# Ten of twelve turns of whole activations moved from TensorE to VectorE blocks and transfers through device memory

## The chip, the core and the metric

The kernel runs on one core of one Trainium2 chip. The metric is the device time of one execution in microseconds (us), the median of three runs. Beside it stands one profiled execution, from which all rows below come. The core has five engines with a queue each: TensorE (PE; its weight loads are PEld), VectorE (DVE), ScalarE (ACT), GpSimd (POOL) and SyncE (SP). Sixteen DMA engines serve the transfers that SP and ACT issue.

## The reference

One encoder layer on x of 256 tokens by 2048 channels, all in f32:

```python
h      = rms_norm(x, g_mix)
z, xbc, dt_f, dt_b, q, k, v, gate_a, gate_b = split(h @ w_in)
y_ssm  = mamba2_bidir(...)        # scans, times silu(z), grouped rms_norm, 2048 channels
y_attn = attention(rope(rms_norm(q)), rope(rms_norm(k)), v)
merged = sigmoid(gate_a) * (y_ssm @ w_ssm_up) + sigmoid(gate_b) * (y_attn @ w_attn_up)
x      = x + merged @ w_out
x      = x + square(relu(rms_norm(x, g_mlp) @ w_mlp_in)) @ w_mlp_out
out    = rms_norm(x, g_final)
```

## The kernel before

**Windows and pieces.** Each product with a weight matrix is cut into windows of 512 output columns. A window has 8 pieces; a piece is 2 of the 16 tiles of 128 input channels. A piece of weights (512 KB) is loaded by SP from device memory into one of 4 slots of `raw` (7 slots in the MLP), split by ACT into a rounded high part `whi` (L637) and by DVE into the rest `wlo` (L1022), and used by PE in three passes (L1719 to L1721) for each of the two blocks of 128 tokens. ACT splits three pieces ahead of PE (`LEAD_HI`), DVE two (`LEAD_LO`). ACT may split into a slot only once PE is done with the piece four before. SP may load into a slot of `raw` once DVE has split what lay there. So all engines keep step with PE piece by piece, with a lead of some pieces.

**Work beside the windows.** `walk` writes out by hand which other work is done beside each window. A function such as `zgate(p, j, ...)` exists once for every engine and is called after piece `p` of the window on that engine, so what it waits for also holds up the weight splits queued behind it on that engine.

**The turns.** PE needs the activations with channels on partitions, while a product gives tokens on partitions. So a whole activation of 256 by 2048 is turned in four rounds of 512 channels. There are three such activations, twelve rounds:

- rounds 0 to 3 (`TS_Z`), in `zgate`: y times silu(z), beside the windows z 1, z 2, z 3 and k;
- rounds 4 to 7 (`TS_MERGED`), in `merged`: the gated sum of the branches, beside attn_up 1, 2, 3 and out 0;
- rounds 8 to 11 (`TS_X2`), in `residual`: the new x, beside out 1, 2, 3 and the first mlp_in window.

A round is eight transposes of 128 by 128 on PE (`transpose_round`, L1740) into the two banks 0 and 1 of the PSUM tensor `S`; then ACT makes the high part out of `S` (`split_high`, L661 and L666) and DVE the low part (`split_low`, L1059 and L1066). The semaphores are `ts_t`, `ts_hi`, `ts_lo`. A consumer window waits on `ts_lo`; the windows out 0 and mlp_in (0, 0) are `late`: they begin with the four channel tiles of the last round missing and wait for that round only before piece 6.

`transpose_round` is also used for q and k in `rope`, for the first conv groups and, in another form, for the attention weights. These stay as they are.

Of the kernel before, what the change touches and what calls it, by code (L numbers as in the profile page):

```python
# [61 lines left out]
FIN_CUTS = (0, 640, FIN, 1664)  # L62

TS_Z, TS_MERGED, TS_X2, TS_END = 0, 4, 8, 12


def walk(eng, window):

    window(0, 0, "xbc", 0, [("rates", 0)])
    window(0, 1, "gate", 0, [("conv", 0), ("decays", 0)])  # L70
    window(1, 0, "xbc", 1, [("scan", 0), ("gate", 0)])
    window(1, 1, "gate", 1, [("conv", 1), ("tables", 0)])
    for i in range(2, GROUPS):
        window(i, 0, "xbc", i, [("gate", i - 1), ("scan", i - 1)])
        window(i, 1, "gate", i, [("conv", i)])
    window(8, 0, "z", 0, [("scan", 7), ("gate", 7)])
    window(8, 1, "z", 1, [("zgate", 0)])
    window(9, 0, "z", 2, [("zgate", 1)])
    window(9, 1, "z", 3, [("zgate", 2)])
    window(10, 0, "k", 0, [("zgate", 3)])  # L80
    window(10, 1, "v", 0, [("rope", 0)])
    window(11, 0, "q", 0, [("values", 0)])
    window(11, 1, "q", 1, [("rope", 1)])
    window(12, 0, "q", 2, [("rope", 2)])
    window(12, 1, "q", 3, [("rope", 3)])
# [12 lines left out]
    window(19, 0, "mlp_in", (0, 0), [("residual", 3)])  # L98

    def pair(g, q, before):  # L100
        window(4 * g + 21 + q, 0, "mlp_pair", (g, q, 0), before)
        window(4 * g + 21 + q, 1, "mlp_pair", (g, q, 1), [("mix_out", (g, q))])

    for g in range(4):
        if g:
            window(4 * g + 19, 0, "mlp_in", (g, 0), [("sums", g - 1), ("mixed", (g - 1, 0))])
        for j in range(1, 4):
            window(4 * g + 19 + j // 2, j % 2, "mlp_in", (g, j), [("hidden", (g, j - 1))] + (
                [("mixed", (g - 1, 1))] if g and j == 1 else []))
# [152 lines left out]
def build(nc, x, x_t, w_in, w_dt, gains_in, taps_in, rows_in, w_ssm_up, w_attn_up, w_out, w_mlp_in, w_mlp_out,  # L262
# [130 lines left out]
    assert top[0] <= nc.sbuf_usable_end, (top[0], nc.sbuf_usable_end)  # L393
    squares_end = nc.alloc_sbuf_tensor_at("squares_end", [P, TB, D], F32, offset=region_a)
    top[0] = region_r
    m_acc1 = nc.alloc_sbuf_tensor_at("m_acc1", [P, 4, N], F32, offset=top[0])
    g_last = place("g_last", [P, D])
    region_f = top[0]
# [42 lines left out]
    expo = sem("expo")  # L441

    ts_t, ts_hi, ts_lo = sem("ts_t"), sem("ts_hi"), sem("ts_lo")
    x_hi, x_lo = sem("x_hi"), sem("x_lo")
    sq_x, var_x, rstd_x = sem("sq_x"), sem("var_x"), sem("rstd_x")
    xt_sq, xt_sum, xt_mm = sem("xt_sq"), sem("xt_sum"), sem("xt_mm")
# [94 lines left out]
        return BLOCK[N_MLP + 8 * PIECES * g + 4 * PIECES + 2 * PIECES * q + PAIR_ORDER[q].index((unit, 3)) + 1]  # L541

    cum_rows = nc.dram_tensor("cum_rows", (2, HEADS, T), F32).ap()

    block = keep.enter_context(nc.Block())

# [85 lines left out]
    def _(act):  # L632
# [6 lines left out]
        def split(m):  # L639
# [13 lines left out]
                act.wait_ge(t_made, turn + SUM_TURN[block])  # L653
            high_part(m, n)

        def split_high(rnd, dst, k0, gain=None, factor=1.0):

            act.wait_ge(ts_t, rnd + 1)
            if gain is None:
                for c in range(2):  # L660
                    last = act.activation(dst[:, ds(k0 + 2 * c, 2), :],  # L661
                                          S[:, c, :].rearrange("p (c t) -> p c t", c=2), ACT.Copy,
                                          scale=factor)
            else:
# [163 lines left out]
        def zgate(p, j, pr, pp):  # L828
            if p == 0:
                act.wait_ge(used, done(pr, pp))  # L830
                if j:
                    act.wait_ge(ts_t, TS_Z + j)
                else:
                    act.wait_ge(off_mm, GROUPS)
                for tb in range(TB):
# [12 lines left out]
            if p == 7:  # L848
                split_high(TS_Z + j, b_hi, 4 * j, gain=2)

        def rope(p, n, pr, pp):
# [59 lines left out]
                last.then_inc(taken[pp], 1)  # L911

        def merged(p, j, pr, pp):
            if p == 2:
                split_high(j + TS_MERGED, b_hi, j * 4, factor=0.5)

        def residual(p, j, pr, pp):
            if p == 2:
                split_high(TS_X2 + j, a_hi, 4 * j, gain=1)
# [59 lines left out]
        table = {f.__name__: f for f in (rates, decays, conv, scan, gate, zgate, rope, values, attend, merged,  # L979
                                         residual, hidden, finish)}  # L980
        between_splits = {f.__name__: f for f in (carry_out, mix_out)}

# [36 lines left out]
    def _(dve):  # L1019
# [7 lines left out]
        def split(m):  # L1027
# [23 lines left out]
            if i > 3:  # L1051
                low_part(m, n + i - 3)

        def split_low(rnd, hi, lo, k0, gain=None, factor=1.0):

            dve.wait_ge(ts_hi, rnd + 1)
            if gain is None:
                for c in range(2):
                    last = dve.scalar_tensor_tensor(  # L1059
# [249 lines left out]
        def zgate(p, j, pr, pp):  # L1309
# [22 lines left out]
            if p == 7:  # L1332
                split_low(TS_Z + j, b_hi, b_lo, 4 * j, gain=2)

        def rope(p, n, pr, pp):
# [13 lines left out]
            if p == 2:  # L1349
                dve.wait_ge(r_root, 2 * (n + 1))  # L1350
                if first(n):
                    dve.wait_ge(ts_t, TS_MERGED)
                else:
                    dve.wait_ge(r_t, n)
                for tb in range(TB):
# [77 lines left out]
        def merged(p, j, pr, pp):  # L1433
            if p == 0:
# [2 lines left out]
                if j == 0:  # L1437
                    dve.wait_ge(r_t, 5)
                else:
                    dve.wait_ge(ts_t, j + TS_MERGED)  # L1440
                dve.tensor_tensor(tmp_b[:, :, :], gates[:, 4 + j, :, :], gates[:, j, :, :], ALU.add
                                  ).then_inc(merge_v, 1)
            if p == 2:
                split_low(j + TS_MERGED, b_hi, b_lo, j * 4, factor=0.5)

        def add_product(j, pr, pp, bank):
# [7 lines left out]
        def residual(p, j, pr, pp):  # L1454
            if p == 0:
                add_product(j, pr, pp, lambda tb: out_product(j, tb))
            if p == 2:
# [98 lines left out]
        def finish(p, j, pr, pp):  # L1556
# [16 lines left out]
        table = {f.__name__: f for f in (rates, decays, conv, scan, tables, zgate, rope, attend, gated_a, merged,  # L1573
                                         residual, hidden, sums, mixed, mix_out, finish)}

        def window(r, par, kind, idx, sides):
# [136 lines left out]
    def _(pe):  # L1713
# [28 lines left out]
            return last  # L1742

        def split_round(rnd, src):
            if rnd:
                pe.wait_ge(ts_lo, rnd)
            transpose_round(src).then_inc(ts_t, 1)


# [104 lines left out]
                                        st_hi[:, 1 - c, :], st_lo[:, 1 - c, :], True, True)  # L1854
                last.then_inc(off_mm, 1)

        def zgate(p, j, pr, pp):
            if p == 6:
                pe.wait_ge(z_v, (j + 1) * Z_V)
                if j == 0:  # L1860
                    pe.wait_ge(scan_v, SCAN_V * GROUPS)
                split_round(TS_Z + j, lambda c, tb: tmp_a[:, tb, c * P:(c + 1) * P])

        def rope(p, n, pr, pp):
            if p == 6:
                pe.wait_ge(r_v, (n + 1) * ROPE_V)
                if n == 0:
                    pe.wait_ge(ts_lo, TS_MERGED)
                else:
                    pe.wait_ge(r_lo, 2 * n)  # L1870
                if n == 4:
# [38 lines left out]
                weigh(p - 4)  # L1910

        def merged(p, j, pr, pp):
            if p == 1:
                pe.wait_ge(merge_v, j + 1)
                pe.wait_ge(at_exp, 8 * KVH)
                split_round(j + TS_MERGED, lambda c, tb: tmp_b[:, tb, c * P:(c + 1) * P])

        def residual(p, j, pr, pp):
            if p == 1:
# [10 lines left out]
        table = {f.__name__: f for f in (rates, decays, conv, scan, zgate, rope, attend, merged, residual)}  # L1930

        def last_window(r, par, idx):

# [99 lines left out]
        def window(r, par, kind, idx, sides):  # L2033
# [139 lines left out]
```

## Time and profile before

| | us |
|---|---|
| median of 3 runs | 1622.51 (1622.29 to 1622.76) |
| span of the profiled execution | 1620.0 |
| PE busy | 1608.5 |
| DVE busy | 1264.1 |
| ACT busy | 917.1 |
| share of the 16 DMA engines, SP's queue | 58.4% |

The profiled execution's own rows cover its span, 1620.0 us from its first to its last instruction; the runs' median is 2.5 us above it. "Busy" of PE is modelled for pipelined matmuls, so it says that PE has work queued and not that it runs at its peak. The DMA share is the mean over the core's sixteen engines.

### The profile page before, as it was taken

The page shows a single profiled execution, that of the slowest core. Times are in us where ns is not written, and L with a number is a line of the kernel's source. Part 1 is how long each engine was busy: PE and PEld are TensorE (multiplying, and loading weights), DVE is VectorE, ACT ScalarE, POOL GpSimd, SP SyncE. Part 2 cuts the span into 40 slices and gives each one's busy share as a digit, 9 for nine tenths or more (in the row PEclk, how much of TensorE's full clock was granted, in tenths as well). Part 3 has the DMA queues.
Part 4 walks back from the last instruction along what each step waited for, and adds up shares of the span by engine and source line. Part 5 has one row for each costly group of instructions (what it writes and reads, how often), then busy time and mean ns, then how long its engine had stood idle before and what let it go on. Part 6 is the DMA issues. An engine that isn't in the chain of part 4 may idle for free.

```text
span 1620.0 us, 20751 instructions
## 1 busy us (share of the span) xinstructions
PE 1608.5 (99%) x8104; PEld 1362.2 (84%) x8104; DVE 1264.1 (78%) x1520; ACT 917.1 (57%) x1262; POOL 79.1 (5%) x67
## 2 busy tenths in 40 slices
PE   9999999999999999999999999999999999999998
PEld 7888888888888888888888888888888888888886
DVE  7888878888666677776665576999799988998893
ACT  6666556666565445544444555665556556655562
POOL 3000000000001134000000000000000000000000
PEclk9999999999999999999999999999999999999999
DMA  7666665666556664445576676458646764586471
GB/s 272 202 200 190 189 200 189 208 195 203 183 186 182 191 187 153 142 145 175 187 229 195 225 236 187 144 182 285 184 125 224 262 190 134 194 282 209 148 245 53
DMA packets 134194, 312.21 MB, mean 193 GB/s; under 512 B 9744, under 2 KB 10448, under 8 KB 133968
## 3 DMA queue, kind: packets, MB, share of 16 engines
q1 hardware_dynamic: 129376, 302.21, 58.4%
q10 hardware_dynamic: 4720, 8.68, 2.0%
q8 instruction: 64, 1.05, 0.3%
q14 instruction: 34, 0.28, 0.0%
HBM read 308.68 MB, written 2.16 MB: 192 GB/s over the span
## 4 chain that ended last, share of the span: by engine, by line
PE 96%; DVE 2%; issue 1%; ACT 0%; POOL 0%; DMA 0%; POOLq 0%; DVEq 0%
PE G L1719 17%; PE G L1720 17%; PE G L1721 17%; PE G L1728 13%; PE S L1728 7%; PE G L1732 6%; PE S L1719 4%; PE S L1721 4%; PE S L1720 4%; PE S L1732 4%; PE S L1740 1%; PE S L1847 1%; DVE wlo L1022 1%; PE S L1891 0%; PE S L1824 0%
## 5 line engine op out<-in xcount | busy, mean ns | idle before, releaser
L637 ACT ACTIVATE whi<-raw 128x1024 fp32r<-128x1024 f32 x395 | 417.0, 1059 | 418.1 <-PE G L1721 254.9
L1022 DVE TENSOR_TENSOR wlo<-raw,whi 128x1024 fp32r<-128x1024 f32 x395 | 482.5, 1236 | 128.7 <-ACT whi L637 127.4
L1719 PE MATMUL G<-whi,a_both 128*128 128x512 f32 x768 | 301.3, 392 | 2.3 <-DVE wlo L1022 1.7
L1721 PE MATMUL G<-whi,a_both 128*128 128x512 f32 x768 | 299.5, 390 | 0.0
L1720 PE MATMUL G<-wlo,a_both 128*128 128x512 f32 x768 | 299.5, 390 | 0.0
L1728 PE MATMUL G<-a_both,whi 128*128 128x512 f32 x640 | 201.7, 397 | 0.0
L1719 PEld LDWEIGHTS G<-whi,a_both 128*128 128x128 f32 x768 | 144.3, 188 | 33.3 <-issue 2.6
L1721 PEld LDWEIGHTS G<-whi,a_both 128*128 128x128 f32 x768 | 144.2, 188 | 30.1
L1720 PEld LDWEIGHTS G<-wlo,a_both 128*128 128x128 f32 x768 | 144.3, 188 | 28.7
L1732 PEld LDWEIGHTS G<-a_both,wlo 128*128 128x128 f32 x640 | 120.3, 188 | 28.2
L1719 PE MATMUL G<-whi,b_hi 128*128 128x512 f32 x342 | 133.9, 392 | 0.0
L1720 PE MATMUL G<-wlo,b_hi 128*128 128x512 f32 x342 | 133.6, 391 | 0.0
L1721 PE MATMUL G<-whi,b_lo 128*128 128x512 f32 x342 | 133.3, 390 | 0.0
L637 ACT ACTIVATE whi_late<-raw 128x1024 fp32r<-128x1024 f32 x85 | 88.9, 1058 | 67.2 <-PE S L1732 22.0
L1732 PE MATMUL G<-a_both,wlo 128*128 128x256 f32 x640 | 125.9, 278 | 0.0
L1022 DVE TENSOR_TENSOR wlo_late<-raw,whi_late 128x1024 fp32r<-128x1024 f32 x85 | 102.6, 1221 | 24.7 <-ACT whi_late L637 24.1
L637 ACT ACTIVATE whi_late<-gates 128x1024 fp32r<-128x1024 f32 x67 | 70.0, 1056 | 49.7 <-PE G L1732 17.9
L1728 PEld LDWEIGHTS G<-a_both,whi 128*128 128x128 f32 x640 | 97.6, 189 | 0.1
L1022 DVE TENSOR_TENSOR wlo_late<-gates,whi_late 128x1024 fp32r<-128x1024 f32 x67 | 81.1, 1221 | 18.7 <-ACT whi_late L637 18.6
L637 ACT ACTIVATE whi<-gates 128x1024 fp32r<-128x1024 f32 x63 | 66.2, 1056 | 38.2 <-PE G L1732 13.9
L1022 DVE TENSOR_TENSOR wlo<-gates,whi 128x1024 fp32r<-128x1024 f32 x63 | 76.3, 1222 | 12.5 <-ACT whi L637 12.0
L1728 PE MATMUL G<-a_both,whi_late 128*128 128x512 f32 x256 | 80.5, 396 | 0.0
(306 smaller groups left out, 2692.4 us busy)
## 6 DMA issues: line engine op xcount, KB each, us to landing
raw<-in_w_in SPq DMA_DIRECT2D x208, 512.0 KB, 4.3
raw<-in_w_mlp_in SPq DMA_DIRECT2D x74, 512.0 KB, 4.0
raw<-in_w_mlp_out SPq DMA_DIRECT2D x74, 512.0 KB, 5.0
gates<-in_w_mlp_in SPq DMA_DIRECT2D x54, 512.0 KB, 4.0
gates<-in_w_mlp_out SPq DMA_DIRECT2D x54, 512.0 KB, 4.9
raw<-in_w_ssm_up SPq DMA_DIRECT2D x32, 512.0 KB, 3.8
raw<-in_w_attn_up SPq DMA_DIRECT2D x32, 512.0 KB, 4.6
raw<-in_w_out SPq DMA_DIRECT2D x32, 512.0 KB, 4.6
```

Source lines behind the costliest of these rows:

```text
L637: act.activation(high(m), piece(n), ACT.Copy).then_inc(hi_made, 1)
L1022: dve.tensor_tensor(low(m), piece(n), high(m).bitcast(F32), ALU.subtract).then_inc(lo_made, 1)
L1719: pe.matmul(out_ap, hi[:, k, cols], w_hi, start=start, stop=False)
L1720: pe.matmul(out_ap, hi[:, k, cols], w_lo, start=False, stop=False)
L1721: return pe.matmul(out_ap, lo[:, k, cols], w_hi, start=False, stop=stop)
L1728: pe.matmul(banks[:, c, :], high(m)[:, cols[kk]], a_both[:, 2 * p + kk, :, :].rearrange("p h t -> p (h t)"), start=(p + kk == 0), stop=False)
L1732: last = pe.matmul(banks[:, c, 0:T], low(m)[:, cols[kk]], a_hi[:, 2 * p + kk, :], start=False, stop=(2 * p + kk == KT - 1))
L1740: last = pe.transpose(S[:, c // 2, c % 2 * T + tb * P:c % 2 * T + (tb + 1) * P], src(c, tb), ident[:, :])
L1847: last = pe.matmul(S[:, 2, (4 * c + h) * HD:(4 * c + h + 1) * HD], mw[:, 0, h, c, :], tm[:, c, h * HD:(h + 1) * HD], start=True, stop=True)
```

## The change

Ten of the twelve rounds leave PE; the last round of `merged` (7) and of `residual` (11) stay. For the ten, DVE turns the 32x32 blocks of the 128x1024 tile in one instruction (`turn_blocks`, into `blocks`). ACT writes `blocks` to device memory in one transfer (`put_blocks`) and, once that has landed, reads it back with the blocks in their turned places in four transfers (`get_blocks`, into `turned_to`, one for each 32 partitions), whose source pieces are runs of 32 f32. `split_high` and `split_low` read `turned_to` in place of `S`. For `merged` and `residual` the order beside one window is: DVE turns at piece 0, ACT puts at 1 and gets at 3, splits high at 6, DVE splits low at 7. For z: DVE turns at 5, ACT puts at 6, and beside the next window (`zturned`) gets at 0, splits high at 3, DVE low at 4. The late windows get one more wait, before piece 4.

```diff
+ON_PE = {rnd: i + 1 for i, rnd in enumerate((TS_MERGED + 3, TS_X2 + 3))}
+BLOCK_ROUNDS = [rnd for rnd in range(TS_END) if rnd not in ON_PE]
+Q = 32
-    window(9, 0, "z", 2, [("zgate", 1)])
-    window(9, 1, "z", 3, [("zgate", 2)])
-    window(10, 0, "k", 0, [("zgate", 3)])
-    window(10, 1, "v", 0, [("rope", 0)])
+    window(9, 0, "z", 2, [("zturned", 0), ("zgate", 1)])
+    window(9, 1, "z", 3, [("zturned", 1), ("zgate", 2)])
+    window(10, 0, "k", 0, [("zturned", 2), ("zgate", 3)])
+    window(10, 1, "v", 0, [("zturned", 3), ("rope", 0)])
...
+    block_rows = nc.dram_tensor("block_rows", (len(BLOCK_ROUNDS), P, TB * N), F32).ap()
+    by_channel = turned_to[:, :, :].rearrange("p (c b) t -> p c (b t)", b=TB)
...
+        def put_blocks(rnd):
+
+            d = BLOCK_ROUNDS.index(rnd)
+            act.wait_ge(blocks_turned, d + 1)
+            act.dma_start(block_rows[d], blocks[:, :, :].rearrange("p b n -> p (b n)")).then_inc(s_put, 16)
+
+        def get_blocks(rnd):
+
+            d = BLOCK_ROUNDS.index(rnd)
+            act.wait_ge(s_put, 16 * (d + 1))
+            if rnd:
+                act.wait_ge(ts_lo, rnd)
+            rows = block_rows[d].rearrange("(i r) (m j w) -> j r m i w", i=4, j=4, w=Q)
+            for j in range(4):
+                act.dma_start(turned_to[Q * j:Q * (j + 1), :, :].rearrange("r m (i w) -> r m i w", i=4), rows[j]
+                              ).then_inc(s_got, 16)
...
         def split_high(rnd, dst, k0, gain=None, factor=1.0):
-            act.wait_ge(ts_t, rnd + 1)
+            if rnd in ON_PE:
+                act.wait_ge(ts_t, ON_PE[rnd])
+            else:
+                act.wait_ge(s_got, 64 * (BLOCK_ROUNDS.index(rnd) + 1))
+                if gain is None:
+                    last = act.activation(dst[:, ds(k0, 4), :], by_channel,
+                                          ACT.Copy, scale=factor)
...
+        def zturned(p, j, pr, pp):
+            if p == 0:
+                get_blocks(TS_Z + j)
+            if p == 3:
                 split_high(TS_Z + j, b_hi, 4 * j, gain=2)
...
         def merged(p, j, pr, pp):
+            if j + TS_MERGED not in ON_PE and p == 1:
+                put_blocks(j + TS_MERGED)
+            if j + TS_MERGED not in ON_PE and p == 3:
+                get_blocks(j + TS_MERGED)
+            if p == (2 if j + TS_MERGED in ON_PE else 6):
+                split_high(j + TS_MERGED, b_hi, j * 4, factor=0.5)
...
+        def turn_blocks(rnd, src):
+
+            d = BLOCK_ROUNDS.index(rnd)
+            if d:
+                dve.wait_ge(s_put, 16 * d)
+            dve.transpose(blocks[:, :, :].rearrange("p b n -> p (b n)").rearrange("p (c b t) -> p c b t", c=4, b=TB),
+                          src.rearrange("p b (c t) -> p c b t", c=4)).then_inc(blocks_turned, 1)
...
-        def zgate(p, j, pr, pp):
-            if p == 6:
-                pe.wait_ge(z_v, (j + 1) * Z_V)
-                if j == 0:
-                    pe.wait_ge(scan_v, SCAN_V * GROUPS)
-                split_round(TS_Z + j, lambda c, tb: tmp_a[:, tb, c * P:(c + 1) * P])
...
                 if p == 0 and rounds is not None:
-                    pe.wait_ge(ready, rounds - 1 if late else rounds)
+                    pe.wait_ge(ready, rounds - 2 if late else rounds)
...
+                if p == PIECES - 4 and late:
+                    pe.wait_ge(ready, rounds - 1)
                 if p == PIECES - 2 and late:
                     pe.wait_ge(ready, rounds)
```

## Rows read from the trace of the kernel before

**Rows 1.** The profile's page: engines, share of the span, and the chain

```profile
PE 1608.5 (99%) x8104; PEld 1362.2 (84%) x8104; DVE 1264.1 (78%) x1520; ACT 917.1 (57%) x1262; POOL 79.1 (5%) x67
...
PE 96%; DVE 2%; issue 1%; ACT 0%; POOL 0%; DMA 0%; POOLq 0%; DVEq 0%
```

**Rows 2.** The chain in order of time: start us, length us, what

```profile
513.84 0.87 PE S L1740 x8
536.50 0.87 PE S L1740 x8
580.91 0.87 PE S L1740 x8
603.56 0.87 PE S L1740 x8
```

**Rows 3.** Line L1740's instructions: duration ns min/median/max, first and last start us

```profile
L1740 PE MATMUL S<-ident,tmp_b x32: 270/272/273, 776.0 to 844.8; 128*128 128x128 f32 x32
```

**Rows 4.** Windows z 3, attn_up 2, out 3: busy us of five engines, PEclk, DMA share, GB/s

```profile
472.10:494.80 22.70, 22.70 (x106) 18.90 (x105) 14.79 (x20) 13.73 (x24) 1.01 (x1) 1.00 0.60 186
793.40:816.10 22.70, 22.70 (x106) 18.89 (x105) 13.42 (x13) 9.46 (x10) 0.00 (x0) 1.00 0.60 191
906.70:929.40 22.70, 22.70 (x106) 18.86 (x105) 12.48 (x14) 11.05 (x16) 0.00 (x0) 1.00 0.72 241
```

**Rows 5.** DMA issues of the page and the DMA view: KB each, us to landing

```profile
raw<-in_w_in SPq DMA_DIRECT2D x208, 512.0 KB, 4.3
raw<-in_w_attn_up SPq DMA_DIRECT2D x32, 512.0 KB, 4.6
...
segs<-cum_rows ACTq DMA_DIRECT2D x16, 512.0 KB, 8.0
...
cum_rows<-cum ACTq DMA_DIRECT2D x1, 64.0 KB, 4.2
```

**Rows 6.** Issue instructions on SP's and ACT's queues: duration ns min/median/max

```profile
L610 SPq DMA_DIRECT2D raw<-in_w_in x208: 327/328/534, 1.2 to 609.6; - x104
...
L610 SPq DMA_DIRECT2D raw<-in_w_attn_up x32: 367/368/368, 729.3 to 819.8; - x32
...
L731 ACTq DMA_DIRECT2D segs<-cum_rows x16: 366/438/2019, 62.4 to 382.1; - x16
```

**Rows 7.** Timeline of ACT and DVE in window z 2, which begins at 449.5 us

```profile
449.59 1.06 ACT L637 ACTIVATE whi<-raw 128x1024 fp32r<-128x1024 f32 x1 [1.09 <-PE G L1721]
...
451.69 1.27 ACT L838 ACTIVATE tmp_b<-G,half_rstd 128x512 f32<-128x512 f32 x2
...
452.99 1.23 DVE L1315 SCALAR_TENSOR_TENSOR tmp_b<-tmp_b,tmp_a 128x1024 f32<-128x1024 f32 x1 [0.53 <-ACT tmp_b L838]
454.25 1.23 DVE L1319 TENSOR_TENSOR tmp_a<-tmp_b,y_sb 128x1024 f32<-128x1024 f32 x1
455.39 2.35 DVE L1022 TENSOR_TENSOR wlo<-raw,whi 128x1024 fp32r<-128x1024 f32 x2
```

**Rows 8.** Timeline of DVE and ACT in window attn_up 1, which begins at 770.8 us

```profile
772.12 1.23 DVE L1441 TENSOR_TENSOR tmp_b<-gates 128x1024 f32<-128x1024 f32 x1
773.26 1.22 DVE L1022 TENSOR_TENSOR wlo<-raw,whi 128x1024 fp32r<-128x1024 f32 x1
...
782.63 1.06 ACT L637 ACTIVATE whi<-raw 128x1024 fp32r<-128x1024 f32 x1 [1.66 <-PE G L1721]
```

**Rows 9.** High and low parts from PSUM (L666, L1066) and from SBUF (L676, L1085)

```profile
L676 ACT ACTIVATE a_both<-gates,gains x16: 492/495/512, 4.2 to 17.0; 128x256 fp32r<-128x256 f32 x16
L1085 DVE SCALAR_TENSOR_TENSOR a_both<-gates,gains,a_both x16: 476/480/485, 5.2 to 18.2; 128x256 fp32r<-128x256 f32 x16
L666 ACT ACTIVATE b_hi<-S,gains x16: 455/468/483, 446.9 to 516.0; 128x256 fp32r<-128x256 f32 x16
L1066 DVE SCALAR_TENSOR_TENSOR b_lo<-S,gains,b_hi x16: 473/477/489, 448.5 to 517.7; 128x256 fp32r<-128x256 f32 x16
```

More of the change, by code:

```diff
@@ L395, in build @@
     top[0] = region_r
+    blocks = nc.alloc_sbuf_tensor_at("blocks", [P, TB, N], F32, offset=region_r)
+    turned_to = nc.alloc_sbuf_tensor_at("turned_to", [P, 2 * 4, P], F32, offset=region_r + 4 * TB * N)
     m_acc1 = nc.alloc_sbuf_tensor_at("m_acc1", [P, 4, N], F32, offset=top[0])
@@ L443, in build @@
     ts_t, ts_hi, ts_lo = sem("ts_t"), sem("ts_hi"), sem("ts_lo")
+    blocks_turned, s_put, s_got = sem("blocks_turned"), sem("s_put"), sem("s_got")
     x_hi, x_lo = sem("x_hi"), sem("x_lo")
@@ L654, in split @@
             high_part(m, n)
-        def split_high(rnd, dst, k0, gain=None, factor=1.0):
-            act.wait_ge(ts_t, rnd + 1)
+        def put_blocks(rnd):
[11 more added lines that the diff above has]
+                              ).then_inc(s_got, 16)
+        def split_high(rnd, dst, k0, gain=None, factor=1.0):
+            if rnd in ON_PE:
[5 more added lines that the diff above has]
+                                          ACT.Copy, scale=factor)
+                else:
+                    for c in range(4):
+                        last = act.activation(dst[:, k0 + c, :], by_channel[:, c, :],
+                                              ACT.Copy, scale=gains[:, gain * KT + k0 + c:gain * KT + k0 + c + 1])
+                last.then_inc(ts_hi, 1)
+                return
             if gain is None:
@@ L831, in zgate @@
                 if j:
-                    act.wait_ge(ts_t, TS_Z + j)
+                    act.wait_ge(blocks_turned, j)
                 else:
@@ L847, in zgate @@
                                        accum_out=z_ss[:, 2 * tb + gg:2 * tb + gg + 1]).then_inc(z_sq, 1)
-            if p == 7:
+            if p == 6:
+                put_blocks(TS_Z + j)
+        def zturned(p, j, pr, pp):
+            if p == 0:
+                get_blocks(TS_Z + j)
+            if p == 3:
                 split_high(TS_Z + j, b_hi, 4 * j, gain=2)
@@ L913, in merged @@
         def merged(p, j, pr, pp):
-            if p == 2:
+            if j + TS_MERGED not in ON_PE and p == 1:
[3 more added lines that the diff above has]
+            if p == (2 if j + TS_MERGED in ON_PE else 6):
                 split_high(j + TS_MERGED, b_hi, j * 4, factor=0.5)
         def residual(p, j, pr, pp):
+            if TS_X2 + j not in ON_PE and p == 1:
+                put_blocks(TS_X2 + j)
+            if TS_X2 + j not in ON_PE and p == 3:
+                get_blocks(TS_X2 + j)
+            if p == (2 if TS_X2 + j in ON_PE else 6):
+                split_high(TS_X2 + j, a_hi, 4 * j, gain=1)
             if p == 2:
-                split_high(TS_X2 + j, a_hi, 4 * j, gain=1)
                 for tb in range(TB):
@@ L977, in finish @@
                     final_squares(j, tb)
-        table = {f.__name__: f for f in (rates, decays, conv, scan, gate, zgate, rope, values, attend, merged,
+        table = {f.__name__: f for f in (rates, decays, conv, scan, gate, zgate, zturned, rope, values, attend, merged,
                                          residual, hidden, finish)}
@@ L1052, in split @@
                 low_part(m, n + i - 3)
+        def turn_blocks(rnd, src):
[4 more added lines that the diff above has]
+                          src.rearrange("p b (c t) -> p c b t", c=4)).then_inc(blocks_turned, 1)
         def split_low(rnd, hi, lo, k0, gain=None, factor=1.0):
             dve.wait_ge(ts_hi, rnd + 1)
+            if rnd not in ON_PE:
+                if gain is None:
+                    part = slice(k0, k0 + 4)
+                    last = dve.scalar_tensor_tensor(
+                        out=lo[:, part, :], in0=by_channel, scalar=factor, in1=hi[:, part, :].bitcast(F32),
+                        op0=ALU.mult, op1=ALU.subtract)
+                else:
+                    for c in range(4):
+                        k = gain * KT + k0 + c
+                        last = dve.scalar_tensor_tensor(
+                            out=lo[:, k0 + c, :], in0=by_channel[:, c, :], scalar=gains[:, k:k + 1],
+                            in1=hi[:, k0 + c, :].bitcast(F32),
+                            op0=ALU.mult, op1=ALU.subtract)
+                last.then_inc(ts_lo, 1)
+                return
             if gain is None:
@@ L1331, in zgate, with zturned @@
                                           ALU.mult, ALU.mult).then_inc(z_v, 1)
-            if p == 7:
+            if p == 5:
+                dve.wait_ge(z_v, (j + 1) * Z_V)
+                turn_blocks(TS_Z + j, tmp_a[:, :, :])
+        def zturned(p, j, pr, pp):
+            if p == 4:
                 split_low(TS_Z + j, b_hi, b_lo, 4 * j, gain=2)
@@ L1351, in rope @@
                 if first(n):
-                    dve.wait_ge(ts_t, TS_MERGED)
+                    dve.wait_ge(blocks_turned, TS_MERGED)
                 else:
@@ L1439, in merged @@
                 else:
-                    dve.wait_ge(ts_t, j + TS_MERGED)
+                    rnd = j - 1 + TS_MERGED
+                    if rnd in ON_PE:
+                        dve.wait_ge(ts_t, ON_PE[rnd])
+                    else:
+                        dve.wait_ge(blocks_turned, BLOCK_ROUNDS.index(rnd) + 1)
                 dve.tensor_tensor(tmp_b[:, :, :], gates[:, 4 + j, :, :], gates[:, j, :, :], ALU.add
                                   ).then_inc(merge_v, 1)
-            if p == 2:
+                if j + TS_MERGED not in ON_PE:
+                    dve.wait_ge(merge_v, j + 1)
+                    turn_blocks(j + TS_MERGED, tmp_b[:, :, :])
+            if p == (2 if j + TS_MERGED in ON_PE else 7):
                 split_low(j + TS_MERGED, b_hi, b_lo, j * 4, factor=0.5)
@@ L1456, in residual @@
                 add_product(j, pr, pp, lambda tb: out_product(j, tb))
-            if p == 2:
+                if TS_X2 + j not in ON_PE:
+                    dve.wait_ge(taken[pp], pr + 1)
+                    turn_blocks(TS_X2 + j, x_sb[:, j, :, :])
+            if p == (2 if TS_X2 + j in ON_PE else 7):
                 split_low(TS_X2 + j, a_hi, a_lo, 4 * j, gain=1)
@@ L1571, in finish @@
                     times_gain(j, tb)
-        table = {f.__name__: f for f in (rates, decays, conv, scan, tables, zgate, rope, attend, gated_a, merged,
+        table = {f.__name__: f for f in (rates, decays, conv, scan, tables, zgate, zturned, rope, attend, gated_a, merged,
                                          residual, hidden, sums, mixed, mix_out, finish)}
@@ L1744, in split_round @@
         def split_round(rnd, src):
-            if rnd:
-                pe.wait_ge(ts_lo, rnd)
+            pe.wait_ge(ts_lo, rnd)
             transpose_round(src).then_inc(ts_t, 1)
@@ L1867, in rope @@
                 if n == 0:
-                    pe.wait_ge(ts_lo, TS_MERGED)
+                    pe.wait_ge(scan_v, SCAN_V * GROUPS)
                 else:
@@ L1912, in merged @@
         def merged(p, j, pr, pp):
-            if p == 1:
+            if p == 1 and j + TS_MERGED in ON_PE:
                 pe.wait_ge(merge_v, j + 1)
@@ L1918, in residual @@
         def residual(p, j, pr, pp):
-            if p == 1:
+            if p == 1 and TS_X2 + j in ON_PE:
                 pe.wait_ge(taken[pp], pr + 1)
@@ L1928, in residual @@
                 last.then_inc(row_mm, 1)
-        table = {f.__name__: f for f in (rates, decays, conv, scan, zgate, rope, attend, merged, residual)}
+        table = {f.__name__: f for f in (rates, decays, conv, scan, rope, attend, merged, residual)}
         def last_window(r, par, idx):
```

## The prediction

> **What bounds the kernel now.** I read the page's engine table and chain first. PE is busy for 99% of the span and 96% of the chain [rows 1]: what leaves PE's stream shortens the kernel as long as nothing makes PE wait in its place. The chain in order of time then prices a round. Rounds follow each other at 22.66 us where each window holds one (513.84 to 536.50); over window v, which holds none, it is 44.41 us (536.50 to 580.91) [rows 2]. So a window without a round takes 44.41 - 22.66 = 21.75 us, 2.72 us a piece, and a round costs PE 0.90 us; its eight transposes last 0.87 us there, 0.27 us each, overlapped [rows 2, 3]. Then I read the windows for what else is full. In a round's window DVE works 13 to 15 us of 22.7 and ACT 9 to 14, and the DMA engines are 60% busy, 72% beside out 3, where loads for the MLP run ahead [rows 4]. The spare time of DMA is the narrowest of the three, and it is there that the change adds most.
>
> **What is removed.** Ten rounds at 0.90 us: 9.0 us of PE, all on the path. 1620.0 - 9.0 = 1611.0 us of span; the median lies 2.5 us above the span, so 1622.5 - 9.0 = 1613.5 us if everything added is hidden.
>
> **DVE.** One block turn of 128x1024 a round. The trace has none. The nearest row is an f32 operation of that size from SBUF to SBUF, 1.23 us [rows 8]; below, nothing; above, I allow twice that, 2.5 us, a stream at half the pace. I take 1.2 us. The high and low parts cost about the same from SBUF as from PSUM (ACT 495 against 468 ns, DVE 480 against 477 [rows 9]), so they are level. DVE goes from at most 14.8 to about 16 us of 21.75. In attn_up 1 the turn comes right behind the sum that ends at 773.35; the split queued behind it (773.26) ends 1.2 us later, at 775.7, and PE needs that piece, the fourth, at 770.8 + 3 x 2.72 = 779.0 [rows 8]. Even 2.5 us hides under the 4.5 us of lead that this piece has now. Turns of z come at piece 5, where only the splits are.
>
> **ACT: issues.** Five a round: one put and four gets. An issue with 128 runs of 4096 B takes 328 ns, one with 256 runs of 2048 B 368 ns, ACT's own with 256 runs 438 ns [rows 6] (the matrices' rows are 512 f32, w_in is laid out so that two rows join; `segs` takes 2048 B runs as well). That is 0.04 us per 128 runs more. A get has 1024 runs: 0.44 + 6 x 0.04 = about 0.7 us as an estimate, 2.7 us for four. The bounds are 0.37 and 2.02 us each (the shortest and longest of ACT's) [rows 6], 1.5 to 8.1 us. In merged and residual they stand at piece 3, ahead of the high part of 782.63, whose piece PE needs only at 770.8 + 7 x 2.72 = 789.8 [rows 8]: less its own 2.3 us for both parts, 4.9 us are free, and 2.7 hide there. The narrow place is z. There the gets stand ahead of zgate's copies: the copies end at 452.96, DVE's two operations of 1.23 us wait for them and end at 455.39, and behind those stands a split whose low part PE needs at 449.5 + 4 x 2.72 = 460.4 and which is done at 456.6 [rows 7]. So 3.8 us of issuing fit there, 2.7 us do. The waits for `s_put` that stand ahead are short: between put and get lie two pieces, 5.4 us, and the one write that the trace shows from ACT, 64 KB, landed in 4.2 us [rows 5].
>
> **DMA: landing.** From the first get to `split_high` lie three pieces, 8.2 us. The nearest rows are the loads of `segs` on the same queue, beside the same weights: 512 KB, 8.0 us to landing [rows 5]. A get that is late holds ACT, and with it all splits queued behind. Working back from PE's need in z: the first get is issued 1.1 us into the window, piece 7 is needed 7 x 2.72 = 19.0 us into it, and before it come, after landing, ACT's part 1.6, DVE's 1.7, zgate's four scalings 1.1 and one low split 1.2: 19.0 - 5.6 - 1.1 = 12.3 us. In merged and residual the first get comes 9.3 us in and the limit is the piece 27.2 us in, with 1.1 + 1.3 + 1.2 us before it: 14.3 us. So a stall of PE begins when four gets take over 12 us.
>
> **DMA: the price of a piece of 128 B.** This decides, and no row shows one. 4096 transfers a round are 256 for each engine. What rows show: in window z 3 the engines were busy 0.60 x 16 x 22.7 = 218 engine-us for 4.22 MB, 1031 packets of 4096 B, 211 ns each. In attn_up 2 it was 218 for 4.34 MB, 2117 packets of 2048 B, 103 ns each [rows 4]. Half the size is half the time, and the fixed part is too small to see, at most some ns. Lower bound: in proportion to the bytes, 6.6 ns, 1.7 us a round. Upper bound: as long as the 2048 B packet, 103 ns, 26 us a round. What fits: the weights of a window take 0.60 x 22.66 = 13.6 us, the put as much as one load, 1.7 us, so of 21.75 us there remain 6.45 us, or 25 ns a packet. For the third round of residual, at 0.72, it is about 15 ns. I take the nearer, lower side, 10 to 20 ns: 2.6 to 5.1 us a round, so the gets land in about 8 us and nothing stalls.
>
> The Trainium skill (DMA: Bandwidth & Descriptors, Specifications) wants at least 512 B for line rate. Read as "a smaller piece costs as 512 B", the gets would move as 2 MB do, by rows 211/8 = 26 ns a packet: right at the limit, the sum about unchanged or a few us worse. Its page VectorE: DVE Perf Modes (The three transpose paths) speaks against the change: a plain copy that turns by strides is "19× slower" than the DMA's own transpose. Here the innermost run is contiguous, 128 B, so I give that rule little.
>
> **The sum.** -9.0 on PE; DVE, ACT and put hidden; gets hidden: 1613.5 us.
>
> **The rivals.**
> 1. *All hidden, 1613.5 us (1612.5 to 1616).* Chance 0.50.
> 2. *Some rounds late.* The price is 20 to 25 ns, or the MLP's early loads collide with round 10. Two to six us are eaten: 1616 to 1619. Chance 0.08. A little more and it is level with before, 1619 to 1626: 0.07.
> 3. *The DMA engines become the bound (the other side).* Place: the ten windows. Beyond 25 ns each ns costs 0.256 us a round. At 45 ns: 13.6 + 1.7 + 11.5 = 26.8 us a window against 22.66, +4.1 us, ten times 41: 1664 us. At 30 ns 1626, at 60 ns 1703. ACT waits for landing, the weight splits stand behind it, PE behind them. For it: the spare share is small. Against: packets in proportion to bytes [rows 4]. Chance 0.24.
> 4. *Strides are ruinous.* At the upper bound, 103 ns, 13.6 + 1.7 + 26.4 = 41.7 us a window: +19, so 1813 us. With 19 times a load's 1.7 us it would be 32 us, +25 a window, 1870. That last figure is what the skill's rule gives. Chance 0.06.
> 5. *Issuing holds ACT.* If a get of 1024 runs blocks ACT as the longest issue did, 2.02 us [rows 6], four take 8.1 us: 4.3 us beyond the 3.8 us in three z windows, 13 us, and 3.2 us beyond the 4.9 us in each of the six others, 19 us: 1622.5 - 9 + 32 = about 1645 us. It decides from about 1 us an issue. Chance 0.05.
>
> **How the numbers follow.** Point: 1613.5, the likeliest case; its own range is 1612.5 to 1616. About 0.2% (3.2 us) is what a measurement of this kernel can tell from no change. Faster: cases 1 and the first of 2, 0.58. Same: 0.07. Slower: 0.24 + 0.06 + 0.05 = 0.35. The range goes up to 1665, which leaves out case 4 and the upper half of case 3, 0.18, and down to 1612.
>
> **What would show it.** Right: PE's transposes at L1740 fall by 80; the chain shows windows of 21.75 us in z, attn_up 1 to 3 and out 1 to 3; the DVE turn is at or under 1.3 us; gets land within 8 us and ACT does not wait for them; the DMA share rises to 0.7 to 0.9 in these windows; the granted clock stays at 1.00, 2.4 GHz. Wrong: ACT's high part waits for a DMA by more than 4 us a round, PE idles behind `wlo`, windows grow beyond 22.66 us with the DMA share near 1.0 (case 3 or 4), or ACT's issue rows are of 1 us and more (case 5). What breaks the prediction is the time of a 128 B packet, above 25 ns.

## The result and the profile after

The changed kernel takes 1633.70 us in the median of five runs (1631.38 to 1639.18), before 1622.51 us. The ratio is 1.0076, interval 1.0062 to 1.0090: slower by 0.8%, where 0.6% faster was forecast. The range, 1612 to 1665, held it, but by luck: it was drawn that wide for case 3, full DMA engines. The case that came nearest is the fifth, issuing holds ACT, to which the prediction gave a chance of 0.05. The profiled execution is the longest of the five, span 1637.2 us, so it shows the effect some 5 us larger than the median. Two later executions, one of e5 (5276 us) and the profiled one of e7 (8938 us), took several times as long as the others of their kernels; they count in no ratio and in no reading, and move e5's and e7's medians by 0.1 us at most.

The page of the changed kernel, answering to [rows 1] (engine table, DMA queues, the chain by engine; q1 is SP's queue, q10 ACT's, each with its packets, MB and share of sixteen engines):

```profile
PE 1608.1 (98%) x8024; PEld 1357.9 (83%) x8024; DVE 1275.1 (78%) x1527; ACT 916.8 (56%) x1259; POOL 79.2 (5%) x67
...
q1 hardware_dynamic: 129376, 302.21, 56.5%
q10 hardware_dynamic: 47760, 19.17, 4.9%
...
PE 89%; DVE 4%; ACTq 2%; DMA 2%; ACT 1%; issue 1%; POOL 0%; POOLq 0%; DVEq 0%
```

PE has 80 instructions less, as it should, yet its share of the chain falls from 96% to 89%. Into its place came DVE, transfers, and "ACTq", ACT's queue issuing transfers. The chain in order of time shows where, in window z 2 (start us, length us, what; rows under 0.1 us are left out):

```profile
443.63 6.70 DMA block_rows<-blocks
450.35 0.66 ACTq L678
451.05 0.70 ACTq L678
451.77 3.17 ACTq L678
454.97 1.95 ACTq L678
...
457.62 0.68 ACT tmp_a L873
458.31 1.17 ACT tmp_b L875 x2
459.49 1.24 DVE tmp_b L1390
460.75 1.24 DVE tmp_a L1394
```

The chain enters through the put, which landed 6.70 us after its issue, 0.02 us before the first get began. L678 is the issue of a get. The first two take 0.66 and 0.70 us, the third 3.17: ACT is held in it. The copies of zgate (L873, L875) come after the fourth, and DVE's two operations, begun at 452.99 in [rows 7], begin at 459.49. Behind them stand the low splits, and PE waited 3.3 us for one, until 463.2. The stretches of the changed kernel show what that does to PE (columns as in [rows 4]):

```profile
450.00:472.00 22.00, 18.66 (x83) 15.12 (x82) 12.95 (x18) 11.95 (x24) 1.01 (x1) 1.00 0.54 151
472.00:500.00 28.00, 22.33 (x89) 17.91 (x88) 15.93 (x21) 13.41 (x24) 1.01 (x1) 0.88 0.67 190
500.00:525.00 25.00, 24.86 (x110) 20.28 (x109) 16.27 (x22) 14.75 (x26) 1.01 (x1) 1.00 0.74 215
525.00:556.00 31.00, 25.90 (x107) 20.64 (x106) 20.60 (x25) 12.08 (x17) 8.44 (x6) 0.91 0.65 185
...
841.00:863.00 22.00, 19.38 (x79) 15.59 (x78) 11.23 (x11) 7.55 (x8) 0.00 (x0) 0.92 0.86 272
...
489.10:495.80 6.70, 4.91 (x12) 3.85 (x13) 5.96 (x10) 5.20 (x14) 1.01 (x1) 0.50 0.56 182
```

PE idles 3.3 us in the first and more than 5 us in the second and fourth, and in these two the granted clock falls from 1.00 to 0.88 and 0.91. The last row shows what lies behind the mean: from 489.1 us on, during and after a wait of 5.7 us, the clock stands at 0.50, 1.2 in place of 2.4 GHz, for 6.8 us. It does so for 3.4 us each from 540.3, 553.9 and 854.3, right after waits of 1.9, 3.2 and 2.6 us. So the idle time costs a good part once more: in z the four long waits are 14.1 us, and the 11.8 us in which PE worked at half the clock cost about 5.9 more. The DMA engines are at 0.54 to 0.74 in these z stretches: they are not full.

The instructions on the new tiles (duration ns min/median/max):

```profile
L668 ACTq DMA_DIRECT2D block_rows<-blocks x10: 326/327/343, 443.6 to 927.5; - x10
...
L1111 DVE STREAM_TRANSPOSE blocks<-tmp_a x4: 1234/1238/1242, 440.4 to 522.4; 128x1024 f32<-128x1024 f32 x4
...
L678 ACTq DMA_DIRECT2D turned_to<-block_rows x40: 564/707/5499, 450.3 to 936.2; - x40
...
DMA to landing us min/median/max: 3.2/6.0/10.7
```

**Where the time went, by stage.** Each kernel has rounds of L1740 (whatever its number there) that are left on PE: rope's second (after z), round 7 (after merged) and round 11 (after residual). Their start in each profiled execution, less that of before, is the balance up to there. These are rows of the chain before (the one after z, 580.91, is in [rows 2]), and of the changed kernel:

```profile
844.16 0.87 PE S L1740 x8
...
934.90 0.87 PE S L1740 x8
```

```profile
598.89 0.87 PE S L1830 x8
...
863.94 0.87 PE S L1830 x8
952.00 0.89 PE S L1830 x8
```

| profiled execution, us against before | after z | after merged | after residual | span |
|---|---|---|---|---|
| all hidden (0.90 a round) | -3.6 | -6.3 | -9.0 | -9.0 |
| changed kernel | +18.0 | +19.8 | +17.1 | +17.2 |
| e1 gets of whole rows | -2.9 | -5.6 | -8.3 | -8.2 |
| e2 two and two | -1.4 | +1.4 | +10.1 | +12.8 |
| e3 gets after the copies | -1.4 | -1.2 | -3.9 | -3.6 |
| e4 z on PE | +0.1 | +4.4 | +1.7 | +1.7 |
| e5 gets on SP | -3.4 | -3.4 | -4.2 | -4.1 |
| e6 order and x spread | -1.4 | +1.0 | -1.7 | -1.6 |
| e8 eight gets | +25.5 | +33.5 | +35.9 | +36.0 |
| e9 gets on SP, x spread | -3.2 | -5.9 | -8.6 | -8.5 |
| e10 runs of 256 B | -1.0 | -0.1 | -1.0 | -0.9 |
| e12 runs of 256 B, order, x spread | -3.2 | -2.4 | -3.3 | -3.2 |

The changed kernel lost 18 + 3.6 = 21.6 us to stalls in z, 1.8 + 2.7 = 4.5 us in merged, and nothing in residual, which gained its full 2.7. The 4.5 us are one round, the third: a wait of 2.6 us until 853.9 and 3.4 us at half the clock. The start of z itself moves by up to 0.4 us between executions.

### The profile page after: what moved, and what is told of

The parts are those of the page before. It is cut to its first block, busy times and chain, and to the rows that moved or that the text cites. A ratio compares the mean times of both kernels' runs of the same rounds, so it can differ in the third digit from the quotient of the medians.

```text
span 1637.2 us, 20655 instructions
## 1 busy us (share of the span) xinstructions
PE 1608.1 (98%) x8024; PEld 1357.9 (83%) x8024; DVE 1275.1 (78%) x1527; ACT 916.8 (56%) x1259; POOL 79.2 (5%) x67
## 4 chain that ended last, share of the span: by engine, by line
PE 89%; DVE 4%; ACTq 2%; DMA 2%; ACT 1%; issue 1%; POOL 0%; POOLq 0%; DVEq 0%
PE G L1809 15%; PE G L1810 15%; PE G L1811 15%; PE G L1818 13%; PE S L1818 7%; PE G L1822 6%; PE S L1809 4%; PE S L1810 4%; PE S L1811 4%; PE S L1822 4%; ACTq L678 2%; DVE wlo L1074 1%; DMA block_rows<-blocks 1%; PE S L1936 1%; PE S L1830 0%
```

## The experiments

All are edits of the changed kernel except e11; their diffs are shown in part. Where a get doesn't move the blocks to their turned places (e1, e10, e12), that part of the result is left out. Ratios are to the kernel before, timed on the same chip.

**e1_long_runs.** Are the bytes and the round trip at fault, or the small pieces?

```diff
-                act.dma_start(turned_to[Q * j:Q * (j + 1), :, :].rearrange("r m (i w) -> r m i w", i=4), rows[j]
+                act.dma_start(turned_to[Q * j:Q * (j + 1), :, :].rearrange("r m t -> r (m t)"),
+                              block_rows[d, Q * j:Q * (j + 1), :]).then_inc(s_got, 16)
```

> The four gets read whole rows of 4096 B in place of runs of 128 B: same bytes, 32 packets a get in place of 1024, same waits and order. The blocks are not moved to their turned places, so this part of the result is left out. Theory A (a get of 1024 runs fills ACT's queue; the third and fourth issue are held until it drains, and the splits queued behind them starve PE): each of the 40 issues takes about 0.33 us, PE waits for nothing, 1612 to 1615 us. Theory B (the round trip through device memory is simply too long, or the added bytes crowd out the weights): the time stays at 1628 us or above.

Measured: 1613.72 us, ratio 0.9946 (0.9931 to 0.9961). The issues:

```profile
L677 ACTq DMA_DIRECT2D turned_to<-block_rows x40: 308/442/637, 449.3 to 908.9; - x40
```

No get is held, and the time is the prediction's sum, 1613.5, within 0.3 us. The removal of ten rounds is worth what [rows 2] say; block turns, puts, waits and 5 MB of gets are hidden. So the whole loss comes with the 1024 runs in a get, not with the bytes or the round trip; the expectation's theory A held.

**e2_two_and_two.** Do two gets fit, and the next two a piece later?

```diff
-            if p == 0:
-                get_blocks(TS_Z + j)
+            if p in (0, 1):
+                get_blocks(TS_Z + j, p)
...
-            if j + TS_MERGED not in ON_PE and p == 3:
-                get_blocks(j + TS_MERGED)
+            if j + TS_MERGED not in ON_PE and p in (3, 4):
+                get_blocks(j + TS_MERGED, p - 3)
...
```

> The four gets of a round are issued two after one piece and two after the next (pieces 3 and 4 in merged and residual, 0 and 1 in z). Theory A (queue full): two gets fit, so the sum of the four issues falls from 4 to 11 us a round to about 3 us, if the first two have drained in 2.7 us; 1612 to 1618 us. Theory B (price of moving small packets beside the weights): held just as long, merely at another piece, 1628 us or above.

Measured: 1630.34 us (1619.18 to 1636.57), ratio 1.0036 (1.0014 to 1.0059). My expectation (1612 to 1618 us) failed: the third get began 1.6 to 3.9 us after the first, and its issue still took 1.6 to 4.4 us in all ten rounds, so 2.7 us is not enough to drain two gets. z nevertheless lost only 2.2 us (table); that part of the hold now stands behind zgate's copies fits this, and e3 tests it. Residual got worse, by 8.7 us where -2.7 was due: the last two gets land later against a `split_high` that stayed at piece 6. ACT's timeline beside out 3:

```profile
917.90 1.30 ACTq L679 DMA_DIRECT2D turned_to<-block_rows  x2
...
921.01 5.36 ACTq L679 DMA_DIRECT2D turned_to<-block_rows  x2
...
936.93 1.70 ACT L693 ACTIVATE a_both<-turned_to,gains 128x256 fp32r<-128x256 f32 x4 [8.45 <-DMA turned_to<-block_rows]
```

ACT waits 8.45 us, until 936.9, for gets whose issue ended at 926.4, and PE waited 9.2 us for the round behind. So there are two losses, held issues and late landing.

**e3_after_copies.** Only the order of the two functions beside z:

```diff
-    window(9, 0, "z", 2, [("zturned", 0), ("zgate", 1)])
+    window(9, 0, "z", 2, [("zgate", 1), ("zturned", 0)])
...
```

and so for the three other windows.

> Only the order in the z windows: zgate's (and rope's) work of a piece comes before the gets of the round before. Theory A with the place in z: the hold of 6 to 9 us no longer delays the copies on which DVE waits with the low splits behind it, but still stands ahead of the next high split. PE needs that split 10.9 us into the window; with 3.4 us before the gets it is late by about 2 us at a hold of 6.6. Of some 21 us lost in z about half come back: 1622 to 1628 us. Rival (order is of no matter, the hold alone counts): 1633 us.

Measured: 1618.73 us (1617.94 to 1624.58), ratio 0.9981 (0.9972 to 0.9990): 15 us better than the changed kernel and level to slightly better than before. The expectation, 1622 to 1628 us, was too high: of 21.6 us lost in z not half but 19.4 came back, and z is at -1.4 in place of +18.0 in the profiled execution. The holds are still there, 4.6 to 6.0 us from the first issue to the end of the last in z (4.4 to 9.3 before), but they cost PE only 2.2 us. What stands behind a held instruction decided most of the loss.

**e4_z_on_pe.** The z rounds back on PE:

```diff
-ON_PE = {rnd: i + 1 for i, rnd in enumerate((TS_MERGED + 3, TS_X2 + 3))}
+ON_PE = {rnd: i + 1 for i, rnd in enumerate((0, 1, 2, 3, TS_MERGED + 3, TS_X2 + 3))}
...
```

with zgate, rope and `walk` as before the change.

> The four rounds of z go back to TensorE, the six of merged and residual stay as changed. Read from the two traces, z lost 17.6 us net, merged 1.8 to 2 us, residual gained 2.7. So 1622.5 - 2.7 + 0 to 2 = 1617 to 1622 us. Rival (the loss is spread over all ten rounds): 1628 us or so.

Measured: 1622.57 us, ratio 0.9999 (0.9989 to 1.0008), 0.6 us above the 1617 to 1622 expected, and not the 1628 us of a loss spread over all rounds. Six rounds less on PE are worth 5.4 us, and all of it is lost again, in the profiled execution all in merged (+4.2 there, where -2.7 was due). One get sequence there lasted 12.1 us.

**e5_sp_gets, e7_sp_gets_x_spread, e9_sp_gets_again.** SP issues the gets, at the place in its order that comes up at the same time; e7 and e9, one kernel, also load x in three separate steps (e9 was run to have a profile of it):

```diff
...
+                for name, at in sides:
+                    if name == "zturned" and p == 7:
+                        get_blocks(TS_Z + at)
+                    if name == "merged" and at and p == 2:
+                        get_blocks(TS_MERGED + at - 1)
+                    if name == "residual" and at and p == 2:
+                        get_blocks(TS_X2 + at - 1)
...
-                if kind == "out" and (idx, p) in ((0, 0), (1, 0)):
+                if kind == "out" and (idx, p) in ((0, 0), (0, 3), (0, 6), (1, 0)):
...
-                    for c in range(3 * idx, 3 + idx):
+                    for c in range(3, 4) if idx else (p // 3,):
```

> The four gets of a round are issued by SP in place of ACT, at the place in SP's order that comes up at about the same time (before the load of piece 7 beside z, of piece 2 of the next window in merged and residual). Same transfers, same packets. Theory A (the loss is ACT held at the issue): SP is held 4 to 10 us a round in its place; its loads have some 4 us of spare and the splits some 5 us of lead behind them, so most of it hides: 1613 to 1619 us. Theory C (the weights' loads themselves are crowded out by the small packets): 1625 us or more, and ACT waits for loads of raw.

> e5_sp_gets and the spread loads of x together. Theory A: 1613 to 1615 us, the nine microseconds of TensorE's rounds whole. Rival: no better than either alone.

> The kernel of e7_sp_gets_x_spread once more, for its interval and a profile. Theory A: 1613 to 1614 us again; SP held 4 to 10 us a round, PE without a wait of over 2 us in the ten windows.

Measured: e5 1617.51 us, ratio 0.9969 (0.9958 to 0.9980); e7 1613.05, ratio 0.9943 (0.9926 to 0.9960); e9 1613.32 (1613.04 to 1613.64), ratio 0.9942 (0.9930 to 0.9955). All three lie in what theory A expected. In e9 (SP's issues of gets, and its timeline in z 2):

```profile
L577 SPq DMA_DIRECT2D turned_to<-block_rows x40: 568/685/4237, 449.1 to 910.5; - x40
...
DMA to landing us min/median/max: 3.2/4.2/6.8
```

```profile
448.68 0.33 SPq L636 DMA_DIRECT2D raw<-in_w_in  x1
449.05 5.59 SPq L577 DMA_DIRECT2D turned_to<-block_rows  x4
454.68 0.68 SPq L636 DMA_DIRECT2D raw<-in_w_in  x1
```

SP is held in these issues for 5.6 us, where ACT was for 6.6; the same packets move, and PE loses nothing: the load behind has the spare time for it. The stretch of e9 about z 2 (columns as in [rows 4]):

```profile
447.80:469.50 21.70, 21.70 (x98) 17.96 (x97) 15.85 (x21) 13.74 (x24) 1.01 (x1) 1.00 0.78 237
```

PE is busy throughout at a clock of 1.00.

**e6_x_loads_spread.** e3's order, and the loads of x spread as above, gets on ACT. Does the longest hold of merged, beside the loads of x, come from these loads?

> The order of e3_after_copies, and the three loads of x (512 KB each) that SP issues at once before out 0 are issued one each before its pieces 0, 3 and 6. Theory A with a collision: the longest holds of merged (10.8 to 12.1 us, against 6.0) fall together with these loads; spread, they come down to 6 or 7 us and the 4 to 5 us lost in merged come back: 1614 to 1616 us. Rival (the long hold has another cause): 1618.7 us as in e3_after_copies.

Measured: 1619.26 us (1614.03 to 1624.51), ratio 0.9977 (0.9964 to 0.9991), as e3. The gets of merged's second and third round were still held 9.0 and 10.4 us; my expectation failed. But the edit did not take the loads of x away from the third round. SP's timeline of e6:

```profile
820.67 0.51 SPq L595 DMA_DIRECT2D gates<-in_x  x1
...
825.01 0.48 SPq L595 DMA_DIRECT2D gates<-in_x  x1
```

They landed at 826.5 and 833.4, and the gets were issued from 822.3 to 832.7. So e6 leaves open what these loads cost on ACT's queue. It does show that they are not the only cause: no load of x was under way beside the second round's 9.0 us. On SP's queue, where e5 and e9 differ in this alone, the spreading is worth 4.2 us (4.5 against e7, timed on e5's chip): in e5 the loads of x stand on the same queue just ahead of the third round, and there already the second get was held, 4.5 us.

**e8_eight_gets.** Each get cut in two of 512 runs:

```diff
-            for j in range(4):
-                act.dma_start(turned_to[Q * j:Q * (j + 1), :, :].rearrange("r m (i w) -> r m i w", i=4), rows[j]
+            for j in range(4):
+                for h in range(2):
+                    at = Q * j + 16 * h
+                    act.dma_start(turned_to[at:at + 16, :, :].rearrange("r m (i w) -> r m i w", i=4),
+                                  rows[j, 16 * h:16 * h + 16]).then_inc(s_got, 16)
...
```

> Each get is cut in two of 512 runs, eight a round, in the order and at the places of the changed kernel. If the queue holds a number of packets (theory A as stated), the first four issues pass at about 0.5 us each and the fifth is the first that is held; if it holds a number of instructions, the third is held. Eight issues add about 1.5 us a round ahead of z's copies: 1633 us or some us more.

Measured: 1654.26 us (two runs), ratio 1.0197 (1.0170 to 1.0225). The chain of e8 in merged's third round (rows under 0.1 us left out):

```profile
853.33 0.56 ACTq L680
853.93 0.89 ACTq L680
854.85 0.72 ACTq L680
855.60 0.73 ACTq L680
856.36 4.30 ACTq L680
860.69 2.40 ACTq L680
```

Four gets of 512 runs pass, the fifth is held: as many runs in flight as with two gets of 1024, 2048, or 128 for each engine. It is so in all six rounds of merged and residual (2.0 to 4.3 us). So packets fill the queue, not instructions. In z it is less clean: in the second round only the eighth is held, and in the third the second already took 1.55 us and the fourth 1.97. I forecast "some us" above 1633 and it was 20: eight issues hold ACT 7.5 to 11.8 us a round, where four took 3.9 to 10.8.

**e10_runs_of_256, e12_256_order_x_spread.** Runs of 64 f32, so 512 packets a get; e12 adds e3's order and the spread loads.

```diff
-            rows = block_rows[d].rearrange("(i r) (m j w) -> j r m i w", i=4, j=4, w=Q)
+            rows = block_rows[d].rearrange("(i r) (m j w) -> j r m i w", i=4, j=4, w=2 * Q)
...
```

> The changed kernel with gets that read runs of 256 B in place of 128 B: same bytes, 512 packets a get in place of 1024, not in the turned places (that part of the result is left out). If the queue holds some 2000 packets (from e8_eight_gets, where the first holds come at the fifth get of 512), all four gets pass nearly free: issues of 0.4 to 1.2 us, and 1613 to 1616 us. If a hold depends on bytes or on the number of gets: as the changed kernel, 1633 us.

> e10_runs_of_256 (gets on ACT, runs of 256 B, blocks not in their turned places) with e3's order in z and the loads of x spread. e10 had no long hold but still lost some 6 us, with gets that landed after up to 14 us and PE waiting in merged for the round before. If that is a collision with the three loads of x at once, it goes away here: 1613 to 1615 us. If it is that ACT's transfers get too small a share of the DMA engines beside SP's queue, as e9_sp_gets_again (largest landing 6.8 us on SP's own queue) suggests, merged stays late: 1617 us or more.

Measured: e10 1620.00 us, ratio 0.9983 (0.9974 to 0.9992); e12 1618.00 (1613.45 to 1618.88), ratio 0.9964 (0.9950 to 0.9978). In e10:

```profile
L678 ACTq DMA_DIRECT2D turned_to<-block_rows x40: 564/658/1507, 449.0 to 916.9; - x40
...
DMA to landing us min/median/max: 3.7/5.9/14.0
```

The long holds are gone (5.5 us to 1.5), which agrees with a queue of about 2000 packets, and 14 us of loss with them. Bytes and the number of gets are those of the changed kernel, so the hold follows neither. One third get of e12 took 2.25 us with only 1024 packets ahead of it, which the count doesn't explain. Neither kernel reached the 1613 to 1615 or 1616 us of my first theories: both still lose in merged, where e12 goes from -3.2 to -2.4, and e12's time is what I expected if merged stays late. Its ACT timeline beside merged's third window:

```profile
835.75 1.06 ACT L688 ACTIVATE b_hi<-turned_to 128x1024 fp32r<-128x1024 f32 x1 [7.26 <-DMA turned_to<-block_rows]
```

Gets issued up to 822.3 have all landed only at 835.7: late landing without a hold. Here too two of the three loads of x, issued at 818.1 and 822.0, fall beside the gets. The stretches of e12 show what the landing waits for (columns as in [rows 4]):

```profile
820.00:825.00 5.00, 5.00 (x24) 4.14 (x23) 2.45 (x2) 1.39 (x2) 0.00 (x0) 1.00 0.94 319
825.00:830.00 5.00, 5.00 (x24) 4.14 (x23) 2.45 (x2) 2.12 (x2) 0.00 (x0) 1.00 1.10 381
```

The DMA engines are full here. By the trace's packet records SP's queue took 1.00 of their time from 821 to 824 us and ACT's 0.01, then 0.86 to 0.88 against 0.20 up to 830. So in this round the gets on ACT's queue waited behind weights and x on SP's. The changed kernel has the same in its third round of merged: a DMA share of 1.07 for 845 to 850 us.

**e11_x_spread_alone.** The kernel before with x spread only.

> Control: the kernel before with the three loads of x spread, nothing else. Theory A: nothing waits for these loads in the kernel before, so 1622.5 us within 0.3. If it gains 1 us or more, that much of e7_sp_gets_x_spread is not due to the gets.

Measured: 1622.49 us, ratio 0.9999 (0.9990 to 1.0008). As expected. Spreading x alone gains nothing, so the 9.4 us of e9 come with the rounds taken off PE.

## Why the prediction failed

**Right.** The gain on PE (9.0 us; e1 has 8.9 and e9 9.4 against their own before). The block turn, 1.24 us where 1.2 was taken. The landing of the gets, 6.0 us in the median. The price of a 128 B piece: q10 gained 43,040 packets and went from 2.0% of 1620.0 us to 4.9% of 1637.2 us of sixteen engines, 765 engine-us; less 1280 packets of 4096 B at 211 ns, 495 are left for 40,960, or 12 ns each. The trace's records of these packets themselves give 13.8 ns in the mean (11 to 68), in the 10 to 20 ns taken and well under the 26 ns of a piece that costs as much as 512 B. Case 4, ruinous strides, did not come, and case 3, engines full, only for some us in the third round of merged; they had 0.30. The Trainium skill's figure of 19 times for a strided copy (VectorE: DVE Perf Modes, The three transpose paths) is stated for a large innermost stride. Here the innermost run is a contiguous 128 B, and the trace shows nothing near it: the busy time of such a packet, 13.8 ns, is about twice its share by bytes, 6.6 ns.

**The step that failed** is "ACT: issues". It extrapolated an issue's time from 128 and 256 runs to 1024, 0.7 us each, 2.7 us for four. That holds for the first and second get (0.56 to 1.2 us) and not beyond. By the trace's packet records all 2048 packets of the first two are still under way when the third begins, in all ten rounds, and its issue takes 1.9 to 5.5 us; in nine of the ten it ends 0.2 to 1.3 us before the first get has landed. So the queue takes some 2000 packets, and the third get waits for the first to drain. Four took 6.6, 9.3, 4.4 and 6.8 us in z, against 3.8 us of room, and 6.0, 6.1 and 10.8 in merged, 3.9 to 4.2 in residual, against 4.9.

The room in z, read from [rows 7], was about right: it gives waits of 2.8 and 5.5 us for the first two rounds, and PE waited 3.3 and 5.7. The room of 4.9 us read from [rows 8] was too small: the rounds of 6.0 and 6.1 us cost PE no wait. z was rightly called the narrow place. What no case had is the clock behind a wait, about 5.9 us in z and 1.7 in merged.

The row to stop at was the longest issue of `segs`, 2.02 us against a median of 0.44 [rows 6]: an issue that can take five times its usual time. It is a warning, not the same thing: it had one other load of 256 packets ahead of it, not 2048. Case 5 used it, as a flat price for each get, and gave 0.05; its sign, issue rows of 1 us and more, is what the profile shows. It came out at about 1645 us against 1633.7 measured. That this is near is in part luck: its price of the stalls, 32 us, of which 19 in merged and residual, compares with 20 in the median run, nearly all in z.

**The second step, smaller:** landing. The sum compared a median (8.0 us) with the room. Single gets landed after up to 10.7 us, and 14 in e10 and e12, mostly in merged's third round. That costs a wait of 3.5 us and 1.7 us at half the clock in each of the two. There the DMA engines were full for some us, which the mean share of a whole window, as in [rows 4], does not show, and SP's queue had most of them. In e9, where SP itself issues the gets and its next loads only behind them, the largest was 6.8 us. How much of it the loads of x make, and by what rule the engines are shared between two queues, is open: no run takes these loads out of that stretch. The puts came late too: the prediction gave them 5.4 us from a single row of 64 KB. The median was 2.8 us, but in z, the narrow place, they took 6.7, 4.0, 5.7 and 5.4 us. That cost little: the first get began 0.25 us after ACT's split had ended, and e1, whose puts took 4.0 to 6.0 us in z, lost at most 0.7 us there.

## What to carry to other kernels

Price a transfer in small pieces by its count as well as by its bytes, and ask what stands behind its issue on that engine: here the same packets cost 20 us ahead of ScalarE's copies, 5 us behind them, and nothing on the queue that had time to spare, once the loads of x were spread. That version, with both edits, takes 1613.3 us and beats the kernel before by 0.6%. An issue's time read at 128 or 256 packets says nothing about one that stands behind 2048. And a mean share of the DMA engines hides the stretch in which they are full.

## What the runs showed of the hardware

- About 2000 packets in flight from one queue, 128 an engine, is where an issue begins to be held: at the third get of 1024 runs in all ten rounds (1.9 to 5.5 us), at the fifth of 512 in merged and residual (2.0 to 4.3 us), never at 32 packets (at most 0.64 us). Some issues took long with less ahead: 1.55 us behind 512 packets in e8, 2.25 us behind 1024 in e12, 2.02 us for one `segs`.
- The issue itself grows little with the count: 0.31 to 0.45 us for 32 packets, 0.33 for 128, 0.56 to 0.7 us for 512 and for 1024.
- A packet of 128 B from device memory kept its DMA engine busy for 13.8 ns in the mean, one of 256 B for 19.7 ns (e10).
- A turn of the 32x32 blocks of a 128x1024 f32 tile on DVE took 1.24 us.
- In or right after waits of PE of 5.7, 1.9, 3.2 and 2.6 us the granted clock stood at 0.50 (1.2 GHz) for 6.8, 3.4, 3.4 and 3.4 us; after one of 3.3 us in the same execution it stayed at 1.00. In e9, with no wait over 1.4 us, it was 1.00 throughout these windows.
